# Where the sums of the weights stand: other quarters of the load buffers, and one place of their own

## The chip, the cores and the metric

One core of a Trainium2 chip runs the whole program in one launch. The metric is the device time in microseconds. The kernel before takes 4246.92 us, the median of three runs (4241.81, 4246.92, 4261.30).

## What is computed

Two model blocks follow each other on 512 tokens of width 1024, in fp32. The second block (two layers) has, per layer, two gated feed-forward stages; they are where the change is. In the reference's words:

```python
def swiglu_2(x, w_gate_up, w_down):
    g, u = jnp.split(x @ w_gate_up, 2, axis=-1)
    return (jax.nn.silu(g) * u) @ w_down
...
h = h + FFN_RES_SCALE * swiglu_2(rms_norm(h, ffa_norm[i]), ffa_w_gate_up[i], ffa_w_down[i])
...
h = h + FFN_RES_SCALE * swiglu_2(rms_norm(h, ffb_norm[i]), ffb_w_gate_up[i], ffb_w_down[i])
```

The hidden width is 2816, so `w_gate_up` is 1024 x 5632 and `w_down` 2816 x 1024. The four stages are called a0, b0, a1 and b1.

## The kernel before

**Arithmetic.** Each fp32 product runs as three matmuls on float32r operands: every operand is split into a rounded high part and a low remainder (hi*hi, hi*lo, lo*hi). The high part of a weight is written by ScalarE (`split_hi`, L438), the low part by VectorE (`split_lo`, L444).

**Seven products for eight.** In a feed-forward stage the gate/up weights are taken in 11 steps c of 256 columns of gate and up. From step S_FFNS on (2 in a0, 1 in the others) a step is a *pair*: the weights form a 2 x 2 block matrix and the activations another, and seven products of sums of blocks replace eight (Strassen's method in Winograd's form). Over the four stages there are 39 pairs. A pair's weights are loaded as two chunks of 1024 KB, the even and the odd one; each has two *quarters* of 512 KB, here e0, e1, o0 and o1. The seven weight pieces, numbered 0 to 6 in the order in which TensorE takes them, are e0, a sum, o0, three sums, o1; the table SUMS = (1, 3, 4, 5) names the sums. PLACE (L129) says for each piece in which quarter, and of which chunk, it stands.

**Who makes the sums.** GpSimd issues DMAs that add their source to their destination (`s_add_pool`, L2822 to L2824). Per pair, `s_ffn_pool` issues four, in this order: piece 1 (e1 += o1, from on-chip memory, once both chunks have landed), piece 4 (e0 += the original e1, read again from HBM, once piece 0 is split), piece 3 (e1 += the original e0, from HBM, once piece 1 is split), piece 5 (e1 += o0, once piece 3 is split). "Split" means that VectorE's low part is done. So pieces 1, 3 and 5 stand one after the other in e1.

**Queues.** SyncE issues the loads of the chunks (`load_chunk`, L424) as their buffer comes free; in the stages there are four buffers, so the next pair is loaded while one is worked on. Both kinds of transfer run on the core's 16 DMA engines. The split weights have room for four pieces, so that piece n+4 is split when the product with piece n is done.

**Order inside a pair.** TensorE (`s_pair_pe`, L2507 to L2509) runs product i as 24 matmuls of 256 columns. The results of products 0, 1 and 3 are copied out of PSUM by ScalarE (`s_keep_act`, L2568, the *keeps*) before products 3, 5 and 4 may add to their banks. So product 4, the fifth, waits for the keep of product 3. Each engine runs its list in order. In ScalarE's list (`s_pair_act`) the keeps stand among the splits, and among the *tail* of the pair before (`s_tail_act`): the last keep, two silu (L2576), two high parts of the gated result (L2581). VectorE has its share of that tail (L2711, L2719, L2725). The split of a pair's piece 3 stands in ScalarE's list ahead of the tail of the pair before:

```python
        if tail and i < 3:
            s_tail_act(k, act, st, c - 1, i)
```

**Parts.** A stage's 11 steps are cut into four parts (S_PARTS: 3, 3, 2, 3 steps), each followed by its share of the down projection (L460 to L462), four chunks of 768 KB or 512 KB. The tail of a part's last pair runs on its own before it. Of the 39 pairs, three (in b0, a1 and b1) open a stage and wait for the activations; 13 more are the first of their part or come right after a whole step; 23 follow another pair.

Of the kernel before, what the change touches and what calls it, by code (L numbers as in the profile page):

```python
# [21 lines left out]
K = 1024  # L22
# [103 lines left out]

PLACE = ((0, 0), (1, 0), (0, 1), (1, 0), (0, 0), (1, 0), (1, 1))  # L129
SUMS = (1, 3, 4, 5)  # L130


# [157 lines left out]
class Kern:  # L290
# [74 lines left out]
    def source(self, u):  # L365
        if u.piece is None:
            return self.raw(u.c)
        return self.quarter(u.c, PLACE[u.piece][0])

    def target(self, slots, u):  # L370
        return self.part(slots, u.c) if u.piece is None else self.factor(slots, u)
# [69 lines left out]
def split_lo(k, dve, n):  # L441
    u = k.W.split[n]
    dve.wait_ge(*k.ev.at(("hi", n)))
    dve.tensor_tensor(k.target(k.wlo, u), k.source(u), k.target(k.whi, u).bitcast(F32), ALU.subtract).then_inc(  # L444
        *k.ev.put("dve_wlo", ("lo", n), *([("raw free", u.c.j)] if u.piece in (None, 5, 6) else [])))


def next_hi(k, act, key):
# [2019 lines left out]
def s_ffn_mem(k):  # L2468
    k.SD = k.two("SD", 32 * K, 6)
    k.TT = k.sb("TT", [128, 4, 4, 2, 256], R0 + 56 * K, F32R)  # L2470
    k.E = [k.sb("E", [128, 2, 2, L], R0 + (88 + 8 * i) * K) for i in range(2)]
    k.ttmp = [k.sb("ttmp", [128, 4, 256], R0 + (96 + 4 * i) * K) for i in range(2)]
    k.dtmp = k.sb("dtmp", [128, L], R0 + 112 * K)

# [121 lines left out]
def s_pair_act(k, act, st, c, tail):  # L2598
    ev, e = k.ev, k.E[c % 2]
    for i in range(7):  # L2600
        if tail and i < 3:
            s_tail_act(k, act, st, c - 1, i)
        if i == 1:
            if c - S_FFNS[st] < 2:
                act.wait_ge(*ev.at(("T", st, 3)))
            p, c0 = s_place(max(0, c - 2))
            if c > 1:
                act.wait_ge(*ev.at(("hd", st, p, 2 * (c - 2 - c0) + 1)))
            if c == S_FFNS[st] > 1:
                act.wait_ge(*ev.at(("hd", st, 0, 2 * c - 1)))  # L2610
        if i in (1, 2, 4):
            act.wait_ge(*ev.at(("mm", st, i - 1, c)))
            s_keep_act(k, act, st, c, i - 1, {1: e[:, 0, :, 0:256], 2: e[:, 1, :, 256:512], 4: e[:, 0, :, 256:512]}[i])
        if i > 0:
            for n in s_freed(k, st, c, i - 1):
                split_hi(k, act, n)
# [205 lines left out]
def s_add_pool(k, pool, u, src):  # L2822

    pool.dma_start(k.source(u), src, accum_op=ALU.add).then_inc(*k.ev.put(f"d_sum{u.piece}", ("sum", u.n), n=16))  # L2824


def s_ffn_pool(k, pool, st):


    ev = k.ev  # L2830
    for c in range(S_FFNS[st], 11):
        even, odd = k.W[(st, "g", c)], k.W[(st, "u", c)]
        p = even.pieces
        pool.wait_ge(*ev.at(("raw", even.j)))
        pool.wait_ge(*ev.at(("raw", odd.j)))
        s_add_pool(k, pool, p[1], k.quarter(odd, 1))
        pool.wait_ge(*ev.at(("lo", p[0].n)))
        s_add_pool(k, pool, p[4], columns(k, even, 1))
        pool.wait_ge(*ev.at(("lo", p[1].n)))
        s_add_pool(k, pool, p[3], columns(k, even, 0))  # L2840
        pool.wait_ge(*ev.at(("lo", p[3].n)))
        s_add_pool(k, pool, p[5], k.quarter(odd, 0))


def hy_mem(k):
# [1368 lines left out]

def ple_sp(k, sp, li):
    ev = k.ev
    sp.wait_ge(*ev.at(("h", ("n7", "n11")[li], 7)))
    sp.dma_start(k.pT[:, :, :], k.I["pT"][li].rearrange("(k p) t -> p k t", p=128)).then_inc(
        *ev.put(f"d_p{li}", ("in", "p", li), n=16))

# [126 lines left out]
def sp_prog(k, sp):  # L4347
# [39 lines left out]
    even_swap_sp(k, sp)  # L4387
    upto(("mo0", 0), 1)
    even_mla_sp(k, sp)
    upto(("b0", "g", 2))  # L4390
    ple_sp(k, sp, 0)
    upto(("fq", 0))
    odd_sp(k, sp)
    upto(("fv", 0), 3)
    odd_mask_sp(k, sp)
    upto(("b1", "g", 2))
    ple_sp(k, sp, 1)
    upto(("pg1", 3), 1)
    assert n[0] == len(W.list)
# [329 lines left out]
```

## Time and profile before

| | |
|---|---|
| median of three runs | 4246.92 us |
| lowest, highest | 4241.81, 4261.30 us |
| the profiled execution | 4246.07 us, of which its span 4244.3 us |
| TensorE busy | 3926.2 us (93%) |
| VectorE, ScalarE, GpSimd busy | 58%, 36%, 15% |
| DMA, mean | 102 GB/s |
| mean granted TensorE clock | 0.959 |

The page sums one execution up: the busy time of each engine, then the chain of work that ended last, followed back from the last instruction. "Busy" on TensorE is modelled from pipelined matmuls. The granted clock is a share of the full 2.4 GHz; 0.5 is 1.2 GHz. GpSimd's DMA issues count as busy there only while it issues. Times in the views are microseconds from the start of the span.

### The profile page before, as it was taken

The numbers are of one execution on the slowest core, as the hardware profiler recorded it, in microseconds if no ns is written. First come the engines' busy times: TensorE is split into PE (matmuls) and PEld (weight loads), VectorE is DVE, ScalarE is ACT, GpSimd is POOL, SyncE is SP. The second block draws the span as 40 slices with busy tenths as digits, with TensorE's granted clock in tenths as the row PEclk, the third lists the DMA queues.
The fourth block names the chain that finished last, engine by engine and source line by source line (L and its number), as shares of the span: only waits on it lengthen the run. The fifth ranks groups of instructions, "written<-read, shape, count | busy, mean of one in ns | idle before, by whom it ended". The sixth has DMA issues, their size and how long they took to land.

```text
span 4244.3 us, 54829 instructions
## 1 busy us (share of the span) xinstructions
PE 3926.2 (93%) x22330; PEld 3357.5 (79%) x22330; DVE 2447.8 (58%) x3609; ACT 1537.9 (36%) x2344; POOL 638.2 (15%) x682
## 2 busy tenths in 40 slices
PE   8998999999999899998989997998899899988988
PEld 5788998888878778887888667888788878678886
DVE  5546656655479953347555645556655563655555
ACT  3235443322333332233334453334433332433333
POOL 0035540100022210011001340011100000010001
PEclk9999999999999999999999998998999999999999
DMA  6210004545311132324564204554255532035551
GB/s 203 93 52 1 1 1 149 158 140 156 98 55 54 51 119 88 104 87 124 141 147 117 65 21 135 146 144 129 84 149 139 138 100 86 11 99 151 128 146 67
DMA packets 286516, 432.98 MB, mean 102 GB/s; under 512 B 12092, under 2 KB 250492, under 8 KB 274749
## 3 DMA queue, kind: packets, MB, share of 16 engines
q1 hardware_dynamic: 263804, 347.70, 25.1%
q0 software_dynamic: 22464, 81.80, 10.5%
q8 instruction: 179, 2.93, 0.3%
q14 instruction: 69, 0.56, 0.0%
HBM read 386.20 MB, written 2.10 MB: 91 GB/s over the span
## 4 chain that ended last, share of the span: by engine, by line
PE 55%; DVE 15%; ACT 8%; issue 6%; DMA 5%; POOL 1%; ACTq 0%; DVEq 0%; SPq 0%; POOLq 0%
PE ps L460 12%; PE ps L462 11%; PE ps L461 11%; ACT whi L438 4%; DVE wlo L444 4%; PE ps L2507 3%; PE ps L2509 3%; PE ps L2508 3%; DMA raw<-in_gu_b 2%; DMA raw<-raw 2%; PE ps L1657 2%; DMA raw<-in_gu_a 1%; ACT E L2568 1%; PE ps L4054 1%; DVE E L2719 1%
## 5 line engine op out<-in xcount | busy, mean ns | idle before, releaser
L444 DVE TENSOR_TENSOR wlo<-raw,whi 128x1024 fp32r<-128x1024 f32 (+4 forms) x500 | 772.7, 1553 | 853.7 <-ACT whi L438 853.6
L438 ACT ACTIVATE whi<-raw 128x1024 fp32r<-128x1024 f32 (+4 forms) x500 | 646.9, 1305 | 1223.0 <-PE ps L462 739.7
L460 PE MATMUL ps<-X,whi 128*128 128x512 f32 x1384 | 551.5, 399 | 14.4 <-DVE wlo L444 8.9
L461 PE MATMUL ps<-X,whi 128*128 128x512 f32 x1384 | 542.6, 392 | 0.0
L2507 PE MATMUL ps<-TT,whi 128*128 128x256 f32 x1248 | 385.1, 309 | 170.0 <-ACT E L2568 121.5
L462 PE MATMUL ps<-X,wlo 128*128 128x512 f32 x1384 | 542.3, 392 | 0.0
L2507 PEld LDWEIGHTS ps<-TT,whi 128*128 128x128 f32 x1248 | 264.2, 212 | 182.3 <-ACT E L2568 132.5
L2509 PE MATMUL ps<-TT,wlo 128*128 128x256 f32 x1248 | 377.4, 302 | 0.0
L2508 PE MATMUL ps<-TT,whi 128*128 128x256 f32 x1248 | 377.4, 302 | 0.0
L460 PEld LDWEIGHTS ps<-X,whi 128*128 128x128 f32 x1384 | 262.3, 189 | 79.4 <-issue 24.8
L460 PE MATMUL ps<-SDh,whi 128*128 128x512 f32 x704 | 281.8, 400 | 33.7 <-DVE wlo L444 15.1
L462 PEld LDWEIGHTS ps<-X,wlo 128*128 128x128 f32 x1384 | 262.2, 189 | 56.1
L461 PEld LDWEIGHTS ps<-X,whi 128*128 128x128 f32 x1384 | 262.4, 190 | 54.9 <-issue 1.4
L461 PE MATMUL ps<-SDl,whi 128*128 128x512 f32 x704 | 277.1, 394 | 0.0
L462 PE MATMUL ps<-SDh,wlo 128*128 128x512 f32 x704 | 276.8, 393 | 0.0
L2507 PE MATMUL ps<-X,whi 128*128 128x256 f32 x936 | 267.8, 286 | 0.0
L2508 PE MATMUL ps<-X,whi 128*128 128x256 f32 x936 | 266.4, 285 | 0.0
L2509 PE MATMUL ps<-X,wlo 128*128 128x256 f32 x936 | 265.7, 284 | 0.0
L2508 PEld LDWEIGHTS ps<-TT,whi 128*128 128x128 f32 x1248 | 265.1, 212 | 0.0
L2509 PEld LDWEIGHTS ps<-TT,wlo 128*128 128x128 f32 x1248 | 264.7, 212 | 0.0
L775 POOL TENSOR_TENSOR sq<-sq,sq 128x512 f32<-128x512 f32 x56 | 80.5, 1437 | 951.6 <-ACT sq L757 951.6
L460 PEld LDWEIGHTS ps<-SDh,whi 128*128 128x128 f32 x704 | 134.0, 190 | 76.5 <-issue 29.5
(626 smaller groups left out, 8093.7 us busy)
## 6 DMA issues: line engine op xcount, KB each, us to landing
raw<-in_ffn_w SPq DMA_DIRECT2D x44, 1024.0 KB, 5.4
raw<-in_gu_a SPq DMA_DIRECT2D x44, 1024.0 KB, 4.8
raw<-in_gu_b SPq DMA_DIRECT2D x44, 1024.0 KB, 5.0
raw<-raw POOLq DMA_DIRECT2D x78, 512.0 KB, 5.2
mslot<-in_mod_w SPq DMA_DIRECT2D x28, 1024.0 KB, 8.1
raw<-in_mod_w SPq DMA_DIRECT2D x20, 1024.0 KB, 6.0
raw<-in_gu_b POOLq DMA_DIRECT2D x40, 512.0 KB, 6.3
raw<-in_gu_a POOLq DMA_DIRECT2D x38, 512.0 KB, 6.4
```

What stands on the lines that cost most here:

```text
L438: act.activation(k.target(k.whi, u), k.source(u), ACT.Copy).then_inc(*k.ev.put("act_whi", ("hi", n)))
L444: dve.tensor_tensor(k.target(k.wlo, u), k.source(u), k.target(k.whi, u).bitcast(F32), ALU.subtract).then_inc(*k.ev.put("dve_wlo", ("lo", n ...
L460: pe.matmul(o, wh, xh, start=first, stop=False)
L461: pe.matmul(o, wh, xl, start=False, stop=False)
L462: return pe.matmul(o, wl, xh, start=False, stop=last)
L775: pool.tensor_tensor(acc, k.sq[0][:, :] if m == 1 else acc, k.sq[m % 2][:, :], ALU.add).then_inc(*k.ev.put("pool_sq", ("sqsum", tag, m)))
L1657: ins = pe.matmul(ps[:, hh * 128:hh * 128 + 128], w(hh), x(hh), start=True, stop=True)
L2507: pe.matmul(o, wh[:, kk, :], xx[:, 0, :], start=first, stop=False, skip_group_check=True)
L2508: pe.matmul(o, wh[:, kk, :], xx[:, 1, :], start=False, stop=False, skip_group_check=True)
L2509: ins = pe.matmul(o, wl[:, kk, :], xx[:, 0, :], start=False, stop=last, skip_group_check=True)
L2568: act.activation(to, k.bk.of((st, PRODUCTS[i][0], c))[:, :].rearrange("p (w t) -> p w t", w=2), ACT.Copy).then_inc(*k.ev.put("act_keep", ( ...
L2719: dve.scalar_tensor_tensor(e[:, m, 0, :], e[:, m, 1, :], (1.0, -1.0)[m], e[:, m, 0, :], ALU.mult, ALU.mult).then_inc(*k.ev.put("dve_ffn", ...
```

## The change

It does four things. The sums stand elsewhere; the fourth (piece 4) is made in a buffer `own4` of 4 KB per partition, which GpSimd first loads with e0 from HBM. With that the waits ahead of the adds are others. ScalarE's keep comes ahead of the tail's step in the first three steps of a pair. And SyncE loads `pT`, which lies in the same memory as `own4`, only after the stage's last piece 4 is split.

```diff
-PLACE = ((0, 0), (1, 0), (0, 1), (1, 0), (0, 0), (1, 0), (1, 1))
+PLACE = ((0, 0), (1, 0), (0, 1), (0, 0), (None, 0), (0, 1), (1, 1))
...
-        return self.quarter(u.c, PLACE[u.piece][0])
+        return self.own4[:, :] if u.piece == 4 else self.quarter(u.c, PLACE[u.piece][0])
...
-        *k.ev.put("dve_wlo", ("lo", n), *([("raw free", u.c.j)] if u.piece in (None, 5, 6) else [])))
+        *k.ev.put("dve_wlo", ("lo", n), *([("raw free", u.c.j)] if u.piece in (None, 6) else [("raw free", u.c.j - 1)] if u.piece == 5 else [])))
...
+    k.own4 = k.sb("own4", [128, 1024], R0 + 114 * K)
...
     for i in range(7):
-        if tail and i < 3:
-            s_tail_act(k, act, st, c - 1, i)
...
             s_keep_act(k, act, st, c, i - 1, {1: e[:, 0, :, 0:256], 2: e[:, 1, :, 256:512], 4: e[:, 0, :, 256:512]}[i])
+        if tail and i < 3:
+            s_tail_act(k, act, st, c - 1, i)
...
         p = even.pieces
+        if c > S_FFNS[st]:
+            pool.wait_ge(*ev.at(("lo", k.W[(st, "g", c - 1)].pieces[4].n)))
+        else:
+            pool.wait_ge(*ev.at(("T", st, 1)))
+        pool.dma_start(k.own4[:, :], columns(k, even, 0)).then_inc(*ev.put("d_own4", ("own4", p[4].n), n=16))
         pool.wait_ge(*ev.at(("raw", even.j)))
         pool.wait_ge(*ev.at(("raw", odd.j)))
         s_add_pool(k, pool, p[1], k.quarter(odd, 1))
+        pool.wait_ge(*ev.at(("own4", p[4].n)))
+        s_add_pool(k, pool, p[4], columns(k, even, 1))
         pool.wait_ge(*ev.at(("lo", p[0].n)))
-        s_add_pool(k, pool, p[4], columns(k, even, 1))
-        pool.wait_ge(*ev.at(("lo", p[1].n)))
-        s_add_pool(k, pool, p[3], columns(k, even, 0))
-        pool.wait_ge(*ev.at(("lo", p[3].n)))
-        s_add_pool(k, pool, p[5], k.quarter(odd, 0))
+        pool.wait_ge(*ev.at(("sum", p[1].n)))
+        s_add_pool(k, pool, p[3], k.quarter(even, 1))
+        pool.wait_ge(*ev.at(("lo", p[2].n)))
+        pool.wait_ge(*ev.at(("sum", p[3].n)))
+        s_add_pool(k, pool, p[5], k.quarter(even, 0))
...
-    sp.wait_ge(*k.ev.at(("h", ("n7", "n11")[li], 7)))
+    sp.wait_ge(*k.ev.at(("lo", k.W[("b%d" % li, "g", 10)].pieces[4].n)))
...
-    upto(("b0", "g", 2))
+    upto(("b0", "d", 3, 0), 2)
     ple_sp(k, sp, 0)
```

So after it: piece 1 is e1 += o1 as before, piece 3 is e0 += e1 (after piece 1's sum), piece 5 is o0 += e0 (after piece 3's sum), and piece 4 is `own4` = e0, then += e1 from HBM. No other instruction is added or taken away.

How it moves the instructions is seen in two places. GpSimd, two pairs in stage b0, before (`raw_55` to `raw_58` are the four buffers, `d_...` semaphores of transfers, `dve_wlo` a low part done):

```order
L2824 DMA raw_58<-raw_57 128x1024 [waits d_raw2,d_raw3]
L2824 DMA raw_58<-in_gu_b 128x1024 [waits dve_wlo] x2
L2824 DMA raw_58<-raw_57 128x1024 [waits dve_wlo]
L2824 DMA raw_55<-raw_56 128x1024 [waits d_raw1,d_raw0]
L2824 DMA raw_55<-in_gu_b 128x1024 [waits dve_wlo] x2
L2824 DMA raw_55<-raw_56 128x1024 [waits dve_wlo]
```

and after (L2839 is the load of `own4`, L2826 the adds):

```order
L2839 DMA own_163<-in_gu_b 128x1024 [waits dve_wlo]
L2826 DMA raw_58<-raw_57 128x1024 [waits d_raw2,d_raw3]
L2826 DMA own_163<-in_gu_b 128x1024 [waits d_own4]
L2826 DMA raw_58<-raw_58 128x1024 [waits d_sum1,dve_wlo]
L2826 DMA raw_57<-raw_58 128x1024 [waits d_sum3,dve_wlo]
L2839 DMA own_163<-in_gu_b 128x1024 [waits dve_wlo]
```

Five transfers a pair instead of four; the one for piece 3 waits for piece 0's low part instead of piece 1's, the one for piece 5 for piece 2's instead of piece 3's, and both for the sum before theirs.

ScalarE, from the split of piece 3 of a pair that follows another to the split of its piece 5, before (`E` is the pair before's buffer, `E_159` this pair's; the keeps are L2568):

```order
L438 ACTIVATE whi_59<-raw_56 128x1024 [waits pe_ffn,d_sum3]
L2568 ACTIVATE E<-ps 128x2x256 [waits pe_ffn]
L2576 ACTIVATE E<-E 128x512 [waits dve_ffn] x2
L2581 ACTIVATE SDh<-E 128x512 [waits dve_ffn]
L2568 ACTIVATE E_159<-ps 128x2x256 [waits pe_ffn,dve_ffn]
L438 ACTIVATE whi_59<-raw_56 128x1024 [waits pe_ffn,d_sum4]
L2581 ACTIVATE SDh<-E 128x512 [waits dve_ffn]
L2568 ACTIVATE E_159<-ps 128x2x256 [waits pe_ffn]
L438 ACTIVATE whi_60<-raw_56 128x1024 [waits pe_ffn,d_sum5]
```

and after:

```order
L439 ACTIVATE whi_59<-raw_56 128x1024 [waits pe_ffn,d_sum3]
L2570 ACTIVATE E<-ps 128x2x256 [waits pe_ffn]
L2578 ACTIVATE E<-E 128x512 [waits dve_ffn]
L2570 ACTIVATE E_159<-ps 128x2x256 [waits pe_ffn,dve_ffn]
L2578 ACTIVATE E<-E 128x512 [waits dve_ffn]
L2583 ACTIVATE SDh<-E 128x512 [waits dve_ffn]
L439 ACTIVATE whi_59<-own_163 128x1024 [waits pe_ffn,d_sum4]
L2570 ACTIVATE E_159<-ps 128x2x256 [waits pe_ffn]
L2583 ACTIVATE SDh<-E 128x512 [waits dve_ffn]
L439 ACTIVATE whi_60<-raw_57 128x1024 [waits pe_ffn,d_sum5]
```

The keep of product 0 now stands between the two silus, the keep of product 1 ahead of the second high part.

## Rows read from the trace of the kernel before

**Rows 1.** The page: the span, and by engine the chain that ended last.
```profile
span 4244.3 us, 54829 instructions
...
PE 55%; DVE 15%; ACT 8%; issue 6%; DMA 5%; POOL 1%; ACTq 0%; DVEq 0%; SPq 0%; POOLq 0%
```

**Rows 2.** TensorE's longest wait over the span: us in total, times, longest us.
```profile
PE ps L2507 <- ACT E L2568: 121.5, 47, 4.2
```

**Rows 3.** Windows, one per pair: the 13 first pairs of a part, and their sum.
```profile
core 0: us, PE busy (x) PEld busy (x) DVE busy (x) ACT busy (x) POOL busy (x), PEclk, DMA share, GB/s
...
3152.03:3173.29 21.26, 20.42 (x170) 20.21 (x169) 13.21 (x14) 9.71 (x11) 3.50 (x4) 1.00 0.72 179
...
sum 309.16, PE 279.53 PEld 276.41 DVE 168.71 ACT 125.97 POOL 42.79; mean PE 21.50 PEld 21.26 DVE 12.98 ACT 9.69 POOL 3.29
```

**Rows 4.** Windows, one per pair: the 23 pairs that follow another, and their sum.
```profile
2694.95:2721.13 26.18, 22.15 (x171) 21.74 (x169) 13.99 (x17) 11.21 (x15) 3.50 (x4) 0.93 0.66 149
...
sum 592.85, PE 506.68 PEld 499.66 DVE 287.00 ACT 232.38 POOL 40.92; mean PE 22.03 PEld 21.72 DVE 12.48 ACT 10.10 POOL 1.78
```

**Rows 5.** ScalarE in order of time, second pair of a part in b0 (start us, us).
```profile
2698.74 1.06 ACT L438 ACTIVATE whi<-raw 128x1024 fp32r<-128x1024 f32 x1 [5.35 <-DMA raw<-in_gu_b]
...
2702.29 0.63 ACT L2576 ACTIVATE E<-E 128x512 f32<-128x512 f32 x1 [1.49 <-DVE E L2711]
...
2703.34 0.58 ACT L2568 ACTIVATE E<-ps 128x512 f32<-128x512 f32 x1
2703.82 1.05 ACT L438 ACTIVATE whi<-raw 128x1024 fp32r<-128x1024 f32 x1
2707.36 0.63 ACT L2581 ACTIVATE SDh<-E 128x512 fp32r<-128x512 f32 x1 [2.50 <-DVE E L2719]
2707.90 0.58 ACT L2568 ACTIVATE E<-ps 128x512 f32<-128x512 f32 x1
2708.38 1.99 ACT L438 ACTIVATE whi<-raw 128x1024 fp32r<-128x1024 f32 x2
2710.27 0.59 ACT L2568 ACTIVATE E<-ps 128x512 f32<-128x512 f32 x1
```

**Rows 6.** TensorE, the same pair: the wait before its fifth product.
```profile
2710.91 0.39 PE L2507 MATMUL ps<-TT,whi 128*128 128x256 f32 x1 [3.80 <-ACT E L2568]
```

**Rows 7.** A window on the product after that wait (columns as in rows 3).
```profile
2710.91:2715.12 4.21, 4.21 (x24) 4.21 (x25) 3.24 (x4) 0.89 (x1) 0.67 (x1) 0.64 0.75 237
```

**Rows 8.** GpSimd (L2824, the adds) in order of time, around that pair.
```profile
2687.65 0.87 POOL L2824 DMA_DIRECT2D raw<-in_gu_b  x1 [8.29 <-DVE wlo L444]
2692.06 0.87 POOL L2824 DMA_DIRECT2D raw<-in_gu_b  x1 [3.55 <-DVE wlo L444]
2701.35 1.76 POOL L2824 DMA_DIRECT2D raw<-raw  x2 [8.42 <-DVE wlo L444]
```

**Rows 9.** VectorE in order of time: subtractions ahead of an add and in that pair.
```profile
2685.00 2.35 DVE L444 TENSOR_TENSOR wlo<-raw,whi 128x1024 fp32r<-128x1024 f32 x2
...
2704.90 1.22 DVE L444 TENSOR_TENSOR wlo<-raw,whi 128x1024 fp32r<-128x1024 f32 x1 [2.65 <-ACT whi L438]
```

**Rows 10.** Windows (columns as in rows 3) during two loads, then during two adds.
```profile
2686.00:2692.00 6.00, 6.00 (x44) 6.00 (x44) 3.27 (x4) 1.06 (x1) 0.87 (x1) 0.82 0.97 328
2692.50:2697.50 5.00, 5.00 (x44) 5.00 (x44) 2.29 (x3) 0.89 (x1) 0.43 (x1) 1.00 1.02 203
```

**Rows 11.** Line L2824 alone: its transfers from issue to landing.
```profile
DMA to landing us min/median/max: 4.5/6.1/9.6
```

**Rows 12.** The page, DMA issues: KB each, median us to landing.
```profile
raw<-raw POOLq DMA_DIRECT2D x78, 512.0 KB, 5.2
...
raw<-in_gu_b POOLq DMA_DIRECT2D x40, 512.0 KB, 6.3
```

**Rows 13.** ScalarE in the first pair of stage b0.
```profile
2575.94 1.06 ACT L438 ACTIVATE whi<-raw 128x1024 fp32r<-128x1024 f32 x1 [11.06 <-DMA raw<-raw]
```

**Rows 14.** TensorE in the first pair of stage b0.
```profile
2578.35 0.55 PE L2507 MATMUL ps<-TT,whi 128*128 128x256 f32 x1 [6.71 <-issue]
```

More of the change, by code:

```diff
@@ L4216, in ple_sp @@
     ev = k.ev
-    sp.wait_ge(*ev.at(("h", ("n7", "n11")[li], 7)))
+    sp.wait_ge(*ev.at(("lo", k.W[("b%d" % li, "g", 10)].pieces[4].n)))
     sp.dma_start(k.pT[:, :, :], k.I["pT"][li].rearrange("(k p) t -> p k t", p=128)).then_inc(
@@ L4395, in sp_prog @@
     odd_mask_sp(k, sp)
-    upto(("b1", "g", 2))
+    upto(("b1", "d", 3, 0), 2)
     ple_sp(k, sp, 1)
```

## The prediction

> **What bounds the kernel now.** I read the page first: over the span, 55% of the chain that ended last is TensorE, and the rest is VectorE, ScalarE, issue and DMA [rows 1]. So TensorE sets the time wherever it isn't made to wait. Then the waits: the largest single one is TensorE on L2507 until a keep of ScalarE is done, 121.5 us in 47 waits [rows 2]. It falls in the pairs, so I cut the stages into one window per pair. A pair is 7 products of 24 matmuls of 0.12 us, 20.2 us of matmuls. The best of the first pairs takes 21.26 us at full clock. The 13 first pairs take 309.16 us, 23.8 each [rows 3]; the 23 that follow another take 592.85 us, 25.8 each [rows 4]. I call 21.3 us the floor of a pair. Above it stand 309.16 - 13 x 21.3 = 32.3 us and 592.85 - 23 x 21.3 = 103.0 us: 135 us is all that better pairs can give.
>
> In time order, one pair shows why. ScalarE is done with everything and waits 5.35 us at 2698.74 for the sum of piece 3 [rows 5]; product 6 of the pair before had ended at about 2695.1 (the pair's window opens at 2694.95 [rows 4]), so the split could have started 3.6 us earlier. From there ScalarE's list runs without slack: the tail of the pair before, the keeps, three more splits, and the keep of product 3 at 2710.27. TensorE waits 3.80 us for it [rows 6]. Then the clock: the product after the wait takes 4.21 us at a mean granted clock of 0.64, so part of it at 1.2 GHz [rows 7], against 2.88 us; the wait is paid again by 1.3 us.
>
> And why is the sum late? Its add is issued at 2692.06, when piece 1 is split, and piece 4's add stands before it at 2687.65 [rows 8]. The first of these comes right behind two splits that end at 2687.35 [rows 9]. One of them and the one just before free the two buffers of the pair that ends, so two chunk loads start there too. The DMA engines are full: 0.97 at 328 GB/s while the loads run, then 1.02 at 203 GB/s while the adds run [rows 10]. An add of 512 KB (0.524 MB) thus takes 2.6 us of all engines, a load of 1024 KB 3.2 us. The shortest add lands 4.5 us after its issue [rows 11]: 1.9 us of it isn't transfer, and I put 1.5 us ahead of it and 0.4 behind (an estimate).
>
> **The change, part by part.** *The order on ScalarE.* Counted from the split of piece 3, the keep of product 3 comes 2710.27 - 2698.74 = 11.5 us later. The keep of product 0 (0.5 us of ScalarE's time) moves into the 1.49 us wait between the silus, the keep of product 1 into the 2.50 us wait before the second high part [rows 5]. The keep of product 3 then comes at 10.5, TensorE starts product 4 at 11.2. Since product 3 ends 11.5 us after the pair's start and its keep takes 0.7 us, this list costs nothing as long as the sum of piece 3 lands no later than 0.9 us after the pair's start.
>
> *The waits before the adds.* The add for piece 3 no longer waits for piece 1's split and comes right after piece 0's, some 3 us earlier against the products; piece 4's add isn't ahead of it any more but far earlier, as soon as `own4` is loaded. What stands in the DMA engines' way is still there. With t = 0 at the pair's start: piece 4 is split at about 7.1 (2704.90 + 1.22 - 2698.74 = 7.4 [rows 5, 9], less 0.5 for the keep, plus 0.2). The load of `own4` is issued at 7.4, the next piece 1's add at 7.9. `own4` transfers from 8.9 to 10.5 (512 KB at the loads' rate, 1.6 us), piece 1 until 13.1, piece 4 (issued 11.2) until 15.7, then the two loads, released at about 11 and 13. The add for piece 3 is issued at 14.7, ready at 16.2. Behind two loads of 1024 KB (6.4 us) it runs from 22.1 to 24.7 and lands at 25.1; the pair could end at 20.9, so it is 4.2 us late. That is the case of 8 of the 23 pairs. In 11 the loads are down weights of 768 KB: 2.6 us late; in 4 they are 512 KB: 1.0. The mean is 2.9, less the 0.9 of slack: 2.0 us above the floor, and 1.1 for the clock (19 of 23 pairs with 1.3): 24.4 us a pair. That is the slow end. The fast end is the floor, 21.3, if the add isn't queued behind the loads. I take **23.6**, nearer to the slow end, because rows 10 show no spare DMA time but a pair that is longer spreads the same loads. Gain 23 x (25.8 - 23.6) = **50 us**; ends 10 (25.4, the `own4` copy at the adds' rate) and 103.
>
> The Trainium skill ("DMA: Bandwidth & Descriptors", Queues, rings and completion order) says that each DMA engine takes turns between the queues it has work for. The rates of rows 10, one after the other, don't look like turns, so the sum above doesn't use it; by that rule the add would share with the loads and land near the pair's end, and all 23 pairs would be at the floor. The same page (Anatomy of one DMA) gives 2.0 us plus bytes over 436 GB/s, 3.2 us for 512 KB; rows 11 have 4.5 at the least, so I go by those; by the page's figure the sum would be the floor as well.
>
> *First pairs.* Here the split pieces come during the down projection, with no loads of the same moment in the way, and the late one is piece 5, whose add had to wait for piece 3's split. It now waits for piece 2's. I expect the floor: **32 us** (bounds: 25 and 32).
>
> *The start of a stage.* In b0, a1 and b1 GpSimd's load of `own4` is issued together with four chunk loads, ahead of piece 1's add, on which ScalarE waits 11.06 us until 2575.94 [rows 13], and TensorE 6.71 us after it [rows 14]. 512 KB more are in front: 1.6 to 2.6 us, three times, **-5 us** (bounds -4 and -8). In a0 the pieces are split ahead, and nothing is lost.
>
> *The rest.* The free signal of the even buffer is given at the same split as before. `pT` is asked for when the last piece 4 is split, a whole pair before its reader in the down projection; the loads behind it on SyncE wait for later splits anyway. If the cover went, one load of some 5 us would show, twice. GpSimd's fifth issue costs it 0.87 us of a pair in which it is idle for most. All at nothing.
>
> Sum: 50 + 32 - 5 = 77 us. The profiled execution took 4246.07 us, 0.85 below the median, so the sum is the same against either: 4246.9 - 77 = **4170 us**.
>
> **Rivals.** *A: everything at the floor.* The adds are served in turn with the loads, as the page has it. For it: the adds' share of the engines is small in later pairs. Against: rows 10. 103 + 32 - 4 = 131 us, 4116 us.
>
> *B: the sum isn't earlier at all.* The fifth transfer takes the place of the one that moved ahead, and piece 3's add still lands last at the same time; only the keeps' 1.0 us a pair remains, and the longer queue eats it. 4247 us, give or take 15. For it: DMA engines at 1.0 in rows 10. Against: one add of 2.6 us less is in front.
>
> *C: slower.* GpSimd's list is in order. Piece 3's add stands behind piece 4's, which waits for `own4` to land, whose load waits for the split of piece 4 of the pair before. That makes a loop: 6.9 us from the split of piece 3 to the end of piece 4's, 0.3 to issue, the landing of `own4`, 0.8 for two issues, the landing of piece 3's add. The pair is 8.0 us plus two landings. With medians of 6.3 and 5.2 [rows 12] that is 19.5, below the floor; with 9.6, the longest [rows 11], twice it is 27.2. Then 23 pairs lose 1.4, the first ones gain nothing, the stages' starts lose 8: 4247 + 32 + 8 = 4287 us. It decides from two landings of 17.8 us together.
>
> **How the numbers follow.** Forecast 0.72, A 0.12, B 0.10, C 0.06. The forecast's own range is from its ends: 10 + 25 - 8 = 27 us (4220) to the floor. The range to hold 8 in 10 takes in A and leaves B, C and the last of the slow end: 4112 to 4216. No change is within 0.5% (21 us), about what a measurement here can tell. Faster: the forecast and A but for its slow tail, and a little of B, 0.84. Same 0.10, slower 0.06.
>
> **What would show it.** In the profile after: the wait of TensorE on L2507's successor for a keep falls from 121.5 to about 60 us; first pairs at 21.3; following pairs at 23 to 24, those of the three-step parts' second longest; ScalarE's split of piece 3 still ended by an add, 1 to 4 us into the pair; fewer fifth products with a granted clock below 1; software DMA up by 20 MB (39 x 0.524); the first pairs of b0, a1 and b1 longer by some 2 us. Wrong would be: piece 3 waiting for nothing (A), GpSimd idle before L2826 until `own4` lands, in pair after pair (C), or the split of piece 3 as late as before (B).

## The result, and the profile after

| | before | after |
|---|---|---|
| median, lowest, highest (four runs each, side by side) | 4249.48, 4241.81, 4261.30 us | 4180.32, 4177.69, 4186.99 us |
| the profiled execution | 4246.07 us | 4177.69 us |
| its span | 4244.3 us | 4175.9 us |

The change makes the kernel faster: the ratio is 0.9837 (95% interval 0.9811 to 0.9863), 69 us less, where 77 us were forecast. The two profiled executions differ by 68.4 us. Their pages and waits are the counterparts of [rows 1, 2, 12]. The page of after, the span, TensorE's and GpSimd's busy time, the software queue (packets, MB, share of the engines), the chain by engine, and the GpSimd transfers with their median from issue to landing:

```profile
span 4175.9 us, 54946 instructions
...
PE 3892.4 (93%) x22330; PEld 3326.6 (80%) x22330; DVE 2447.7 (59%) x3609; ACT 1540.7 (37%) x2344; POOL 659.9 (16%) x721
...
q0 software_dynamic: 28080, 102.25, 11.9%
...
PE 54%; DVE 16%; DMA 7%; ACT 7%; issue 4%; POOL 0%; DVEq 0%; ACTq 0%; SPq 0%; POOLq 0%
...
raw<-raw POOLq DMA_DIRECT2D x117, 512.0 KB, 5.7
...
own<-in_gu_b POOLq DMA_DIRECT2D x40, 512.0 KB, 6.8
own<-in_gu_a POOLq DMA_DIRECT2D x38, 512.0 KB, 6.3
```

What TensorE waits for, after (total us, times, longest):

```profile
PE ps L2509 <- ACT E L2570: 81.8, 41, 5.5
```

The keep's wait has lost 121.5 - 81.8 = 39.7 us, not the 60 of the forecast, and its longest case has grown from 4.2 to 5.5 us. TensorE is busy 33.8 us less for the same matmuls (more of them run at full clock, see the end); DMA's share of the chain is 7% (5% before). The software queue carries 20.45 MB more (81.80 before), the 39 loads of `own4`.

Then one window per pair, as in [rows 3, 4]. After, the sum line of the 13 first pairs, then of the 23 that follow another, then one that follows another in b0 and stands for the pair of [rows 5]:

```profile
sum 275.97, PE 265.70 PEld 262.73 DVE 168.91 ACT 129.13 POOL 50.03; mean PE 20.44 PEld 20.21 DVE 12.99 ACT 9.93 POOL 3.85
...
sum 560.90, PE 492.32 PEld 486.68 DVE 291.96 ACT 232.64 POOL 51.47; mean PE 21.41 PEld 21.16 DVE 12.69 ACT 10.11 POOL 2.24
...
2671.84:2698.33 26.49, 22.49 (x171) 22.29 (x169) 14.00 (x17) 11.20 (x15) 4.06 (x5) 0.87 0.71 154
```

The first pairs go from 309.16 to 275.97 us, the following ones from 592.85 to 560.90, the three that open a stage from 127.8 to 126.9, and all that lies outside the pairs is 2.4 shorter: 33.2 + 31.9 + 0.9 + 2.4 = 68.4 us. By kind, from the same windows, in the mean us of one pair:

| kind (number) | before | after |
|---|---|---|
| first of its part (13) | 23.78 | 21.23 |
| second of a three-step part, 1024 KB loads (8) | 26.38 | 26.61 |
| third of it, 768 KB (8) | 24.91 | 22.11 |
| second pair of a stage, 768 KB (3) | 26.77 | 28.33 |
| second of a two-step part, 512 KB (4) | 25.55 | 21.52 |
| opening a stage (3) | 42.6 | 42.3 |

So all of the gain lies in 25 pairs. The other 11 (second of a three-step part, second of a stage) have gained nothing; together they take 6.5 us more than before. One of these, in time order. GpSimd's issues after for that pair, the second of its part, from the load of `own4` to the add for piece 5:

```profile
2656.99 0.55 POOL L2839 DMA_DIRECT2D own<-in_gu_b  x1 [2.33 <-DVE wlo L445]
2657.53 0.91 POOL L2826 DMA_DIRECT2D raw<-raw  x1
2661.02 0.89 POOL L2826 DMA_DIRECT2D own<-in_gu_b  x1 [2.59 <-DMA own<-in_gu_b]
2665.55 0.87 POOL L2826 DMA_DIRECT2D raw<-raw  x1 [3.65 <-DVE wlo L445]
2676.82 0.87 POOL L2826 DMA_DIRECT2D raw<-raw  x1 [10.39 <-DMA raw<-raw]
```

SyncE's two chunk loads of 1024 KB each:

```profile
2660.67 2.06 SPq L425 DMA_DIRECT2D raw<-in_gu_b  x2
```

ScalarE's split of piece 3, the keeps and the splits behind it (the last row is the keep of product 3):

```profile
2676.31 1.06 ACT L439 ACTIVATE whi<-raw 128x1024 fp32r<-128x1024 f32 x1 [6.03 <-DMA raw<-raw]
...
2678.28 0.59 ACT L2570 ACTIVATE E<-ps 128x512 f32<-128x512 f32 x1
2679.87 0.63 ACT L2578 ACTIVATE E<-E 128x512 f32<-128x512 f32 x1 [1.00 <-DVE E L2713]
...
2681.87 0.58 ACT L2570 ACTIVATE E<-ps 128x512 f32<-128x512 f32 x1
2684.46 0.63 ACT L2583 ACTIVATE SDh<-E 128x512 fp32r<-128x512 f32 x1 [2.01 <-DVE E L2721]
2685.00 1.99 ACT L439 ACTIVATE whi<-raw 128x1024 fp32r<-128x1024 f32 x2
2686.89 0.58 ACT L2570 ACTIVATE E<-ps 128x512 f32<-128x512 f32 x1
```

TensorE's start on the fifth product, the counterpart of [rows 6]:

```profile
2687.52 0.58 PE L2509 MATMUL ps<-TT,whi 128*128 128x256 f32 x1 [4.00 <-ACT E L2570]
```

And windows of after (columns as in rows 3) during these transfers, then on that fifth product:

```profile
2664.00:2672.00 8.00, 8.00 (x69) 8.00 (x68) 5.52 (x6) 2.12 (x2) 0.87 (x1) 1.00 0.98 290
2672.00:2676.00 4.00, 4.00 (x36) 4.00 (x35) 0.14 (x1) 0.00 (x0) 0.00 (x0) 1.00 0.54 114
...
2687.52:2692.58 5.06, 5.06 (x25) 5.06 (x26) 3.25 (x4) 0.89 (x1) 1.75 (x2) 0.53 0.93 195
```

Read together: the add for piece 3 is issued at 2665.55, 6.3 us *before* its pair begins at 2671.84, and still its split starts 4.5 us into the pair, because the transfer takes 10.7 us from issue to landing. Two things are in its way: the chunk loads issued from 2660.67 on, and piece 4's add, issued at 2661.02, which takes 12.5 us itself. Before the change the same add was issued at 2692.06, 2.9 us before its pair, and landed in 6.7. Issuing earlier was answered by landing later. The keep of product 3, which ends TensorE's wait, starts 10.6 us after piece 3's split (11.5 before), so the move in ScalarE's list has done its part.

### The profile page after: what moved, and what is told of

Same layout as the page of the kernel before. It is cut to its first block, busy times and chain, and to the rows that moved or that the text cites. A ratio compares the mean times of both kernels' runs of the same rounds, so it can differ in the third digit from the quotient of the medians.

```text
span 4175.9 us, 54946 instructions
## 1 busy us (share of the span) xinstructions
PE 3892.4 (93%) x22330; PEld 3326.6 (80%) x22330; DVE 2447.7 (59%) x3609; ACT 1540.7 (37%) x2344; POOL 659.9 (16%) x721
## 4 chain that ended last, share of the span: by engine, by line
PE 54%; DVE 16%; DMA 7%; ACT 7%; issue 4%; POOL 0%; DVEq 0%; ACTq 0%; SPq 0%; POOLq 0%
PE ps L461 12%; PE ps L463 12%; PE ps L462 12%; DMA raw<-raw 6%; DVE wlo L445 4%; ACT whi L439 4%; PE ps L2509 2%; PE ps L2511 2%; PE ps L2510 2%; PE ps L1658 2%; DVE E L2721 1%; PE ps L4062 1%; DVE SDl L2727 1%; DVE E L2713 1%; PE ps L4049 1%
## 5 line engine op out<-in xcount | busy, mean ns | idle before, releaser
L445 DVE TENSOR_TENSOR wlo<-raw,whi 128x1024 fp32r<-128x1024 f32 (+4 forms) x461 | 725.2, 1581 | 745.6 <-ACT whi L439 745.5
L439 ACT ACTIVATE whi<-raw 128x1024 fp32r<-128x1024 f32 (+4 forms) x461 | 605.7, 1326 | 1142.1 <-PE ps L463 739.8
L2509 PE MATMUL ps<-TT,whi 128*128 128x256 f32 x1248 | 372.6, 299 | 132.7 <-ACT E L2570 81.8
L2509 PEld LDWEIGHTS ps<-TT,whi 128*128 128x128 f32 x1248 | 252.7, 202 | 143.6 <-ACT E L2570 90.3
L2510 PE MATMUL ps<-TT,whi 128*128 128x256 f32 x1248 | 366.0, 293 | 0.0
L2511 PE MATMUL ps<-TT,wlo 128*128 128x256 f32 x1248 | 365.6, 293 | 0.0
L461 PE MATMUL ps<-SDh,whi 128*128 128x512 f32 x704 | 281.1, 399 | 33.8 <-DVE wlo L445 15.1
L2510 PEld LDWEIGHTS ps<-TT,whi 128*128 128x128 f32 x1248 | 253.1, 203 | 0.0
L2511 PEld LDWEIGHTS ps<-TT,wlo 128*128 128x128 f32 x1248 | 252.8, 203 | 0.0
L2826 POOL DMA_DIRECT2D raw<-raw x117 | 102.1, 873 | 943.2 <-DVE wlo L445 325.9
```

The lines of the kernel that those rows point to most:

```text
L439: act.activation(k.target(k.whi, u), k.source(u), ACT.Copy).then_inc(*k.ev.put("act_whi", ("hi", n)))
L461: pe.matmul(o, wh, xh, start=first, stop=False)
L2509: pe.matmul(o, wh[:, kk, :], xx[:, 0, :], start=first, stop=False, skip_group_check=True)
L2510: pe.matmul(o, wh[:, kk, :], xx[:, 1, :], start=False, stop=False, skip_group_check=True)
L2511: ins = pe.matmul(o, wl[:, kk, :], xx[:, 0, :], start=False, stop=last, skip_group_check=True)
```

## The experiments

Two theories stood at first. **The queue**: what is left in the following pairs is the time that piece 3's add spends among the chunk loads. **The chain**: it is GpSimd's list (each transfer behind the wait of the one before), or ScalarE's, whatever the DMA engines do. All kernels were timed against the kernel before, measured at the same time; "us a pair" is from windows, one per pair, as above.

### Later loads, e4

The change, but SyncE does not load into the buffers of a pair until piece 3's sum of the next pair in the part has landed:

```diff
 def load_chunk(k, sp, c):
...
+    if c.before is not None and c.before in k.pair_of:
+        st, x = k.pair_of[c.before]
+        if x < 10 and s_place(x) == s_place(x + 1):
+            sp.wait_ge(*k.ev.at(("sum", k.W[(st, "g", x + 1)].pieces[3].n)))
...
+    k.pair_of = {k.W[(st, w, c)].j: (st, c) for st in S_FFNS for c in range(S_FFNS[st], 11) for w in "gu"}
```

> The changed kernel in which SyncE, before it loads into a buffer of a pair, also waits for the sum of piece 3 of the next pair in the same part, so that the two chunk loads no longer stand ahead of that add. Theory: the add lands 1 to 2 us before the pair's start, and the 11 late pairs (26.6 and 28.3 us on average) come down to 21.5 to 23 us, while the add of piece 5 now stands behind the loads and costs up to 1 us: 40 to 50 us less than the changed kernel, 4130 to 4140 us. Rival (GpSimd's own order, or own4, sets the add): no change, 4178 to 4185. Second rival (the loads come too late for the next pair's first pieces): slower than 4185, with ScalarE waiting for chunk loads.

Measured: 4122.83 us, ratio 0.9696 (0.9679 to 0.9712): 57 us below the change, more than expected. TensorE's waits, then the eight second pairs of three-step parts (sum line), then the 23 following pairs:

```profile
PE ps L2513 <- ACT E L2574: 39.5, 39, 3.9
```

```profile
sum 174.31, PE 164.78 PEld 163.15 DVE 111.75 ACT 92.98 POOL 32.31; mean PE 20.60 PEld 20.39 DVE 13.97 ACT 11.62 POOL 4.04
...
sum 502.54, PE 474.89 PEld 469.85 DVE 287.17 ACT 240.58 POOL 51.39; mean PE 20.65 PEld 20.43 DVE 12.49 ACT 10.46 POOL 2.23
```

The second pairs of three take 174.31 / 8 = 21.8 us (26.6 in the change), the following pairs 21.85 in the mean. In order of time in e4, the pair that begins at 2661.79: GpSimd's adds for pieces 3 and 5, SyncE's two loads, and ScalarE's splits:

```profile
2655.52 0.87 POOL L2830 DMA_DIRECT2D raw<-raw  x1 [3.54 <-DVE wlo L449]
2661.79 0.87 POOL L2830 DMA_DIRECT2D raw<-raw  x1 [5.40 <-DVE wlo L449]
```

```profile
2660.41 0.80 SPq L429 DMA_DIRECT2D raw<-in_gu_b  x2
```

```profile
2662.05 1.06 ACT L443 ACTIVATE whi<-raw 128x1024 fp32r<-128x1024 f32 x1 [1.81 <-PE ps L2515]
...
2671.23 2.01 ACT L443 ACTIVATE whi<-raw 128x1024 fp32r<-128x1024 f32 x2 [0.39 <-DMA raw<-raw]
```

The add for piece 3 now lands in 4.8 us, and its split waits for TensorE alone. The delay hasn't vanished: piece 5's add is now the one among the loads and takes 9.4 us. But it is issued at the pair's start and its split is due 9 us later, so of the delay 0.39 us is seen. The price was moved to where there is slack. The second pairs of the three stages keep part of it: they take 24.8 us (28.3 in the change).

### More bytes in the queue, e3

The change with one more copy of 512 KB from HBM to HBM in each pair, behind the load of `own4`. No engine reads it. GpSimd waits for the copy of the pair before to land ahead of issuing the next; the trace has no idle time there.

```diff
         pool.dma_start(k.own4[:, :], columns(k, even, 0)).then_inc(*ev.put("d_own4", ("own4", p[4].n), n=16))
+        if ("extra", st, c - 1) in ev.value:
+            pool.wait_ge(*ev.at(("extra", st, c - 1)))
+        elif k.last_extra:
+            pool.wait_ge(*ev.at(k.last_extra))
+        k.last_extra = ("extra", st, c)
+        pool.dma_start(k.extra[:, :], columns(k, even, 0)).then_inc(*ev.put("d_extra", ("extra", st, c), n=16))
```

> The changed kernel with one more transfer of 512 KB per pair, from HBM to a scratch place in HBM that nobody reads, issued by GpSimd right behind the load of own4. Theory (the DMA engines' queue makes the sum of piece 3 late in a pair that follows one at the floor): it puts 1.3 to 2.6 us more ahead of that sum, so the 11 pairs that are late now grow by that each, the first pairs stay at 21.1 to 21.9, in all 20 to 45 us more: 4200 to 4225 us. Rival (GpSimd waits for own4 to land, and that sets the add): the copy comes behind own4, so the pairs stay as they are but for 0.9 us of issue: 4180 to 4190.

Measured: 4217.47 us, ratio 0.9915 (0.9900 to 0.9930), 37 us above the change. The first pairs stay at 21.2 us; the second of three go from 26.6 to 28.0, the third from 22.1 to 23.6, the second of two from 21.5 to 22.4, and the opening ones from 42.3 to 43.8. The queues (packets, MB, share), and GpSimd's transfers into `own4` in stages b0 and b1 (20 loads and 20 adds together; 6.8 us in the change), in e3:

```profile
q0 software_dynamic: 33696, 122.70, 13.2%
...
own<-in_gu_b POOLq DMA_DIRECT2D x40, 512.0 KB, 7.7
```

A transfer whose data no engine uses costs time in just the pairs that have loads in the way, and none in those without. GpSimd's one further issue can't be told apart here from the bytes; but the first pairs have that issue too.

### Piece 3's add first, e5, and both, e6

The order of the adds of pieces 3 and 4 in GpSimd's list is exchanged.

```diff
         s_add_pool(k, pool, p[1], k.quarter(odd, 1))
-        pool.wait_ge(*ev.at(("own4", p[4].n)))
-        s_add_pool(k, pool, p[4], columns(k, even, 1))
         pool.wait_ge(*ev.at(("lo", p[0].n)))
         pool.wait_ge(*ev.at(("sum", p[1].n)))
         s_add_pool(k, pool, p[3], k.quarter(even, 1))
+        pool.wait_ge(*ev.at(("own4", p[4].n)))
+        s_add_pool(k, pool, p[4], columns(k, even, 1))
```

> The changed kernel with GpSimd's adds for pieces 3 and 4 exchanged. Theory (what is queued ahead of piece 3's add makes it late): one add of 2.6 us less is ahead of it, piece 4's comes 2.6 us after it and isn't wanted before 4.6 us after the split of piece 3. The late pairs (second of three 26.6, second of a stage 28.3 us) lose 2.6 us of wait and partly the slow clock: 23 to 25. 25 to 45 us less than the changed kernel: 4138 to 4158 us. Rival (the two loads alone make it late): 4175 to 4185.

Measured: 4131.94 us, ratio 0.9711 (0.9685 to 0.9736). In the counterpart of the pair shown, the add for piece 3 takes 7.5 us instead of 10.7, and the second pairs of three take 23.0 us. So the other half of the obstacle was the add ahead of it in GpSimd's own queue. Piece 4 can afford it: it is split 4.6 us after piece 3.

e6 puts e4 and e5 together.

> The loads later and piece 3's add first together. Theory: with the loads out of the way the pairs outside the stages' starts are at 21.1 already except the second of a stage (24.8) and a few others; these are what is left to gain, 5 to 15 us below the kernel with the loads later (4122.83): 4108 to 4120 us. If piece 4's add now comes behind the loads it may be late instead: then no gain or up to 10 us slower.

Measured: 4137.57 us, ratio 0.9734 (0.9715 to 0.9753). The expected further gain is not there: e6 isn't told from e5, and it is slower than e4, whose interval ends at 0.9712. The profiled execution is e6's fastest (4121.25 us; the others took 4134 to 4142), so its span of 4119.4 us, against e4's 4118.9, hides that. Its following pairs of three-step parts take 22.4 and 21.5 us, 21.8 and 21.2 in e4. Each of the two edits takes queueing out of piece 3's path, and what one has taken the other doesn't take again; why both together are slower than the later loads alone isn't shown. The lowest median of all kernels is e4's, the change with later loads, 129 us below the kernel before measured beside it (4251.78).

### The same wait in the kernel before, e7 and e11

If the loads are in the way, the same wait ahead of SyncE's loads should help the kernel before. e7 has e4's edit and nothing of the change.

> The kernel before (its places, its waits, its order on ScalarE) with nothing but SyncE's wait for the sum of piece 3 of the next pair. Theory (queue and waits add up): without the loads piece 3's add lands 4.5 us after it is issued, but it is issued only when piece 1 is split, 3 us before the pair's start, so it is 1.6 us late in every following pair; these take 23 to 24.5 us instead of 25.8, the first pairs stay at 23.8. 30 to 60 us less than before: 4190 to 4222 us. Rival 1 (the queue is all of it, the places needn't change): 4120 to 4150. Rival 2 (the queue matters only with the change's fifth transfer): 4240 to 4255.

Measured: 4251.27 us, ratio 1.0005 (0.9993 to 1.0017). Nothing: the second pairs of three take 27.3 us (26.4 before), and what other pairs gain makes up for it. This was the surprise of the study. TensorE's waits in e7, then GpSimd, ScalarE and TensorE in the pair that begins at 2696.40:

```profile
PE ps L2511 <- ACT E L2572: 118.5, 39, 5.3
```

```profile
2693.52 0.87 POOL L2828 DMA_DIRECT2D raw<-in_gu_b  x1 [3.41 <-DVE wlo L448]
2701.46 0.86 POOL L2828 DMA_DIRECT2D raw<-raw  x1 [7.07 <-DVE wlo L448]
```

```profile
2698.85 1.06 ACT L442 ACTIVATE whi<-raw 128x1024 fp32r<-128x1024 f32 x1 [4.00 <-DMA raw<-in_gu_b]
...
2709.95 2.00 ACT L442 ACTIVATE whi<-raw 128x1024 fp32r<-128x1024 f32 x2 [1.36 <-DMA raw<-raw]
```

```profile
2712.49 0.39 PE L2511 MATMUL ps<-TT,whi 128*128 128x256 f32 x1 [4.41 <-ACT E L2572]
```

The add for piece 3 lands in 5.3 us, as it should, but it can't be issued before piece 1 is split, so its split is 2.4 us into the pair anyway. And piece 5's add can't be issued before piece 3 is split: at 2701.46, 5.1 us into the pair, behind the two loads that piece 3's landing has just released (2698.90). It takes 8.5 us. In e4 the same add is issued at the pair's start. The queueing was handed from one link of the chain to the next. The time is that of the second rival, but its reason (the queue matters only with the fifth transfer) doesn't fit these rows: without a fifth transfer the add for piece 3 lands in 5.3 us instead of 6.7.

e11 holds the loads back until piece 5's sum, so that no add of the pair is behind them (against e7):

```diff
-            sp.wait_ge(*k.ev.at(("sum", k.W[(st, "g", x + 1)].pieces[3].n)))
+            sp.wait_ge(*k.ev.at(("sum", k.W[(st, "g", x + 1)].pieces[5].n)))
```

> The kernel before, in which SyncE's two loads wait for the sum of piece 5 of the next pair instead of piece 3's. In the run with piece 3's (4251.27 us) piece 5's add stood behind the loads and landed 8.5 us after its issue. Theory: now both adds are free of the loads, the following pairs come to 23 to 24.5 us, if the loads aren't then too late for the next pair (they are wanted some 8 us after they start): 4200 to 4230 us. Rival (the loads were never what held the kernel before): 4245 to 4255 again. Second rival: too late, slower than 4255, with ScalarE waiting for chunk loads.

Measured: 4251.73 us, ratio 0.9992 (0.9976 to 1.0009). The second pairs of three improve from 26.4 to 24.9 us, and the third worsen from 24.9 to 28.2, for now the loads are late themselves. ScalarE in e11, the third pair's splits of piece 1 (with the one behind it) and of piece 3:

```profile
2718.94 2.01 ACT L442 ACTIVATE whi<-raw 128x1024 fp32r<-128x1024 f32 x2 [8.13 <-DMA raw<-raw]
2726.96 1.06 ACT L442 ACTIVATE whi<-raw 128x1024 fp32r<-128x1024 f32 x1 [6.01 <-DMA raw<-in_gu_b]
```

The loads are issued from 2704.87 on and the later one lands 8.2 us after its issue; piece 1's add can go only at 2714.07, 9.2 us after the first issue (it takes 4.8 us), and behind it piece 3's. So in the kernel before none of the three places tried for the loads was good: too early they hold up an add, too late the next pair. It is the change's shorter chain that makes room for them.

### The parts of the change, e1, e2, e9, e10, e12

e1 is the kernel before with only the new order in ScalarE's list; e2 is the change with the old one.

```diff
-        if tail and i < 3:
-            s_tail_act(k, act, st, c - 1, i)
...
+        if tail and i < 3:
+            s_tail_act(k, act, st, c - 1, i)
```

> The kernel before with ScalarE's order alone changed (keeps ahead of the tail). Theory (the sum of piece 3 starts ScalarE's list, the list is then 1.0 us shorter): each of the 36 pairs outside the stages' starts gets about 1.0 us shorter where it was above 21.3, so some 30 us less: 4215 to 4225 us. Rival 1 (the order is most of the gain): 4180 to 4195. Rival 2 (the order gives nothing, since the next sum is late by as much): 4245 to 4252.

> The changed kernel with ScalarE's old order. Theory: first pairs of a part keep nearly all of their gain, because no tail stands in them; pairs that follow another lose about 1.0 us each, 23 us: about 4200 to 4206 us. Rival 1 (the places alone make the gain): 4178 to 4185. Rival 2 (the order made most of it): above 4230.

Measured, against 4251.78 us: e1 4228.51 us, ratio 0.9943 (0.9929 to 0.9958); e2 4200.61 us, 0.9878 (0.9864 to 0.9893). The order is worth 23 us alone, less than the 30 that were expected of e1, and the places (with their waits) 51 alone; together they give 69, so they share little. In e1's windows the following pairs take 19.9 us less, 0.9 each where the forecast had 1.0, and the first ones 5.5 less.

e9 is the change, but piece 3's add waits for piece 1's split again; e10, piece 5's add for piece 3's split again; e12 has both waits.

```diff
+        pool.wait_ge(*ev.at(("lo", p[1].n)))
         s_add_pool(k, pool, p[3], k.quarter(even, 1))
...
+        pool.wait_ge(*ev.at(("lo", p[3].n)))
         s_add_pool(k, pool, p[5], k.quarter(even, 0))
```

> The changed kernel, with the add for piece 3 waiting again for the split of piece 1, as in the kernel before. Theory: in the first pairs the two splits are 1.1 us apart, so these stay; in the second pairs the add stands behind the loads anyway and stays; in the third ones and the second of two steps it is issued 3 us later and lands up to 2 us late: 0 to 1 us each. 5 to 20 us more than the changed kernel: 4185 to 4200. Rival (this wait is most of what the change gained): 4220 to 4250.

> The changed kernel, with the add for piece 5 waiting again for the split of piece 3. Theory: the add is issued 2.6 us after that split starts and lands 4.5 to 6.5 us later, just before ScalarE asks for it at 8.7, so pairs stay within 0.5 us: 0 to 15 us more, 4180 to 4195. Rival (the chain through piece 5 made the first pairs late, as the prediction says): the first pairs go back up by 1 to 2.6 us, 4195 to 4230.

> The changed kernel with both waits back, piece 3's add after piece 1's split and piece 5's after piece 3's, as in the kernel before: what is left of the change is the fourth sum's own place, its earlier add, and ScalarE's order. Theory (piece 4's add out of the way of piece 3's is the larger part): the first pairs stay below 22, in all 4195 to 4215 us. Rival (the two waits are most of it, either alone being hidden by the other): near the kernel before with ScalarE's order changed, 4220 to 4232.

| | median us | ratio (95%) | first pairs, us | following, us |
|---|---|---|---|---|
| the change | 4180.32 | 0.9837 (0.9811 to 0.9863) | 21.2 | 24.4 |
| e9, first wait back | 4192.27 | 0.9862 (0.9817 to 0.9907) | 21.1 | 24.8 |
| e10, second wait back | 4199.94 | 0.9870 (0.9830 to 0.9911) | 21.3 | 24.7 |
| e12, both back | 4216.10 | 0.9923 (0.9900 to 0.9945) | 22.2 | 25.1 |

The two waits together are worth some 36 us. The intervals of e9 and e10 overlap the change's, so what one wait costs alone isn't told by the times. e10's median is above the range expected for it, and lies in that of its rival, but the first pairs didn't grow as the rival had it. e12's lies between its expected range (up to 4215) and its rival's (from 4220). The pairs are the surer measure, since outside of them, where these edits change nothing, e9's profiled execution is 12 us shorter than the change's and e12's 13 us longer; inside the pairs e12 is 35 us longer. In the first pairs neither wait alone costs anything (21.1, 21.3) and both cost 1.0 us each pair: with one link loose the chain of pieces 1, 3 and 5 seems to have slack again. What remains in e12 against the kernel before is 34 us. If the order is worth there what it is in e1, some 11 are left for piece 4's early add in a place of its own; that share wasn't measured by itself.

### The start of a stage, e8

e4, with the load of `own4` behind piece 1's add in the first pair of each stage.

```diff
-        else:
-            pool.wait_ge(*ev.at(("T", st, 1)))
-        pool.dma_start(k.own4[:, :], columns(k, even, 0)).then_inc(*ev.put("d_own4", ("own4", p[4].n), n=16))
+            own()
...
         s_add_pool(k, pool, p[1], k.quarter(odd, 1))
+        if c == S_FFNS[st]:
+            pool.wait_ge(*ev.at(("T", st, 1)))
+            own()
```

(`own()` issues the same load.)

> The kernel with the loads later, and in the first pair of each stage the load of own4 behind piece 1's add. Theory (at a stage's start own4's 512 KB stand ahead of piece 1's add): TensorE's wait before the second product of these pairs, 7.2, 7.9 us and the like, goes back to 6.5 to 6.7 us as in the kernel before; 2 to 4 us less than the kernel with the loads later, 4118 to 4122 us, hardly to be told by the time alone. Rival (own4 isn't in the way there): the waits stay.

Measured: 4125.14 us, ratio 0.9700 (0.9683 to 0.9717), not to be told from e4 by its time. In the windows the three opening pairs go from 42.1 to 41.6 us, and TensorE's wait before their second product from 7.2, 7.9 and 7.3 us to 6.8, 7.2 and 6.8 (6.5 to 6.7 were expected), so the load in front costs about 0.5 us each, a third of the 1.6 that the forecast gave it at the least.

## Why the prediction was right, and which term was mis-sized

**Direction and main path held, and the sum in part by luck.** 4170 us was forecast, 4180 measured, inside the range. The piece that is late, what makes it late and what ScalarE's new order gives were read rightly. But the sum of 77 us is 8.6 above the profiled 68.4 because two misses cancel in part: 18 us too much for the following pairs, and 9.5 too little for all else (the stages' starts 5.9, what lies outside the pairs 2.4, the first pairs 1.2).

**First pairs, -32 us: measured -33.2.** The size is right, and they are at the floor of 21.3 us. The reason given, that piece 5's add had to wait for piece 3's split, was incomplete: with that wait back alone (e10) they stay at 21.3, with both waits back (e12) they take 22.2, and the remaining 1.5 us to 23.8 is not from a wait that these runs separate, so its cause stays open; e1 shows that the order isn't most of it (23.4).

**Following pairs, -50 us: measured -32. This is the mis-sized term, and the step that failed is the choice of 23.6 between the ends.** The working of the slow end was right almost to the digit. It had piece 3's add issued at 14.7 us (2665.55, with the pair before beginning at 2650.75: 14.8) and its split 4.2 us late (4.5). By kind it gives 21.3 + 3.3 + 1.3 = 25.9 us behind 1024 KB loads (measured 26.6), 21.3 + 1.7 + 1.3 = 24.3 behind 768 KB (the two kinds, (176.91 + 84.98) / 11 = 23.8), and 21.4 behind 512 KB (21.5): 24.4 in the mean, and 560.90 / 23 = 24.39 was measured. That the middle kind fits is luck: its 23.8 is the mean of eight pairs at 22.1 and three at 28.3. The step from 24.4 to 23.6 rested on "a pair that is longer spreads the same loads", which no row showed. Had the sum gone by 24.4, it would have been 32 + 32 - 5 = 59 us, about as far below the 68.4 as 77 is above.

**One statement in that working is wrong without harming the sum.** Piece 4's add was said not to be ahead of piece 3's any more; its transfer was put at 13.1 to 15.7 us, done before the loads. It is issued at 10.3 us, 4.5 us ahead of piece 3's, but takes 12.5 us and lands at 22.8, about when the second load does. Piece 3's add has the same bytes to wait for either way, so its landing came out nearly right (25.1; 25.5 measured). What the statement hid is that the order of the two adds was worth changing: e5 took off 48 us by it.

**The pair that gained nothing** was forecast as the worst ("the three-step parts' second longest"), but not as no better than before; there the saved wait in the list was used up in the queue in full. Against the forecast of 25.9 this kind is 0.7 us longer, and most of that is the clock: 1.3 us were allowed for it, and the fifth products of the eight pairs take 4.73 us in the mean (the one shown above 5.06, at a granted clock of 0.53) against 2.97 at full clock, 1.8 more.

**The order on ScalarE.** The keep of product 3 was put 10.5 us behind the split of piece 3, and is 10.6. e1 gives the order's worth in the kernel before.

**The start of a stage, +5 us: measured -0.9.** TensorE's wait of [rows 14] did grow, from 6.71 us; the same row of after:

```profile
2557.89 0.55 PE L2509 MATMUL ps<-TT,whi 128*128 128x256 f32 x1 [7.44 <-issue]
```

0.7 here, and 2.1 and 0.5 in the other two stages, 3.4 in all. What the forecast left out is that the same pairs gain later: their wait before the fifth product shrinks by 0.1, 1.9 and 1.7 us. The term took the loss of the move and not its gain in the same pair.

**The rest at nothing** held. `pT` lands 5.4 us after its issue and is read 24 us after it.

**Rivals.** B (nothing) and C (slower, by the loop through `own4`) are refuted by the time. C's sign is there: GpSimd waits 2.6 us for `own4` in the pair shown, and 66.9 us in 24 waits over the whole span. But the loads of `own4` alone take 3.8 us in the median (the 6.3 and 6.8 of the page are of loads and adds together), and the two landings in the pair shown are 3.7 and 10.7 us, 14.4 together where C needed 17.8. A is half seen. The DMA queues of after from 2665.6 to 2672 us (packets, MB, share of the engines), with GpSimd's queue first:

```profile
q0 software_dynamic: 174, 0.66, 53.0%
q1 hardware_dynamic: 168, 1.16, 49.1%
```

Here the adds and the loads share the engines, half and half. The two loads take 8.4 and 11.7 us (4.8 and 7.0 before), and the adds for pieces 4 and 3 take 12.5 and 10.7. The Trainium skill ("DMA: Bandwidth & Descriptors", Queues, rings and completion order) says that an engine takes turns between the queues it has work for. This stretch of the trace agrees, with 53.0% and 49.1%.

Rows 10 looked otherwise for a reason that the traces also show: an add that is issued when loads run or have just been issued moves nothing at first. Before, from 2684.5 to 2691.6, the queue of the adds has no packet, although one was issued at 2687.65; by then the loads were nearly through. After, there is none from 2662.9 to 2665.7, with an add issued at 2661.02, and in e4 none up to 2666.7, with one issued at 2661.79. So the first packet comes 4 to 5 us after the issue beside loads, and in e7, in a pair without loads beside it, 1.5 us after it (issued at 2693.52, none up to 2695.0). What causes this delay isn't shown.

Sharing doesn't bring the pairs to the floor, as A had it: it makes every one of the transfers long, and piece 3's add is the last of them, behind piece 4's. That piece 4's add in front counts is shown by e5, and that the loads count by e4.

**The wait of TensorE** was said to fall to about 60 us and fell to 81.8, by the same mis-sized term.

## What to carry to other kernels

A transfer that is issued earlier lands earlier only if nothing fills the DMA engines between: count, at its new time of issue, the bytes already asked for, and take the sum that comes out. Where bulk loads are free to start as soon as a buffer is, let them wait for the small transfer that the next step needs; here one such wait on top of the change took off 57 us more, and the same wait in the kernel before took off none, because there the next link of a chain of waits was due at once. So loosen the chain first, then place the loads, and try each part alone and together, since effects that hide each other don't add.

## What the runs showed that was not expected

**One add, four durations.** 512 KB from issue to landing took 4.5 us at the least, 7.5 with the adds exchanged (e5), 10.7 in the change, 12.5 for the add next to it. What differs between them in the trace is what had been asked for in the 5 us before and the 10 us after.

**The clock is a large part of a wait's price.** The fifth products of the 39 pairs, one window each, sum line of the kernel before:

```profile
sum 159.65, PE 159.60 PEld 159.62 DVE 97.18 ACT 20.59 POOL 12.61; mean PE 4.09 PEld 4.09 DVE 2.49 ACT 0.53 POOL 0.32
```

and of after:

```profile
sum 137.40, PE 137.34 PEld 137.38 DVE 82.89 ACT 20.59 POOL 20.38; mean PE 3.52 PEld 3.52 DVE 2.13 ACT 0.53 POOL 0.52
```

The work is the same, and 22 of the pairs' 66 us come from here: 28 of the 39 products ran at 1.2 GHz in part or in full before, and 12 do after. It isn't told by the wait's length alone. In after, two of them, each behind a wait for a keep (windows, columns as in rows 3):

```profile
2070.47:2074.94 4.47, 4.47 (x25) 4.47 (x26) 2.11 (x3) 0.00 (x0) 0.00 (x0) 0.62 0.73 232
2245.90:2248.88 2.98, 2.98 (x24) 2.98 (x25) 2.12 (x3) 0.00 (x0) 0.00 (x0) 1.00 0.03 5
```

The first follows a wait of 1.73 us and runs partly at 1.2 GHz, the second one of 2.46 us and runs at full clock. The forecast charged 1.3 us to 19 of the 23 following pairs, 25 us; measured are 21 us, in 12 pairs, 1.8 us each. The sum is near because too many waits were charged too little each.
